# Output stage of an encoder layer: output products cut into quarters, with the transposes, routing and affinities of a tile between them

## The reference, cut to what matters

```python
    mixed = jnp.concatenate([out_a, out_b], axis=-1)
    x = x + jnp.matmul(mixed, w_o)
    x = x + expert_choice_moe(rmsnorm(x, norm2), w_router, w_gate, w_up, w_down)
...
    cap = CAPACITY_FACTOR * n_tok // N_EXPERTS
    aff = jax.nn.softmax(jnp.matmul(xt, w_router).astype(jnp.float32), axis=-1)
    gate, idx = lax.top_k(aff.T, cap)
    xg = xt[idx]
    h = jax.nn.silu(jnp.einsum('ecd,edf->ecf', xg, w_gate)) * jnp.einsum('ecd,edf->ecf', xg, w_up)
    y = jnp.einsum('ecf,efd->ecd', h, w_down) * gate[..., None].astype(x.dtype)
```

## Time and profile before

| | |
|---|---|
| median of 3 runs | 1774.64 us (1774.34 to 1776.37) |
| span of the profiled execution | 1773.7 us |
| PE busy in it | 1728.7 us, 97% |
| DVE, ACT, POOL busy | 1186.7, 1074.0, 388.9 us |
| mean clock granted to PE | 0.988 |

### The profile page before, as it was taken

How to read it: one execution, slowest core, us unless ns; L and a number is a source line. 1 busy time by engine, 2 the same in 40 slices (tenths; PEclk the granted TensorE clock), 3 DMA queues, 4 the chain that set the end, 5 groups by cost and what they waited for, 6 DMA issues and landing times.

```text
span 1773.7 us, 30258 instructions
## 1 busy us (share of the span) xinstructions
PE 1728.7 (97%) x10582; PEld 1576.8 (89%) x10582; DVE 1186.7 (67%) x2358; ACT 1074.0 (61%) x2140; POOL 388.9 (22%) x552
## 2 busy tenths in 40 slices
PE   9999999899999999999999999999999999999995
PEld 9789898799998878888899999999999999999994
DVE  4442533488888973137778777787777877778776
ACT  4333333388888983333466666666666666666665
POOL 1322402254445542221100111001110011100112
PEclk9999999899999999999999999999999999999998
DMA  7556645654544743334786786777867777777775
GB/s 236 125 160 202 192 126 153 161 165 149 149 147 134 208 117 127 110 107 152 253 271 245 267 272 226 263 251 266 269 228 259 256 266 258 239 254 260 267 265 227
DMA packets 203485, 367.13 MB, mean 207 GB/s; under 512 B 39055, under 2 KB 64655, under 8 KB 202831
## 3 DMA queue, kind: packets, MB, share of 16 engines
q1 hardware_dynamic: 190268, 320.92, 54.1%
q0 software_dynamic: 13120, 44.96, 9.9%
HBM read 321.67 MB, written 50.45 MB: 210 GB/s over the span
## 4 chain that ended last, share of the span: by engine, by line
PE 47%; DVE 2%; DMA 2%; ACT 1%; POOL 1%; issue 0%; DVEq 0%; SPq 0%; ACTq 0%; POOLq 0%
PE psum L2158 21%; PE psum L2160 10%; PE psum L2177 3%; PE psum L2178 3%; PE psum L2179 3%; PE psum L2180 3%; PE psum L2181 3%; PE psum L2143 1%; DMA own_rows<-x 1%; DMA x<-y_s,index 0%; DVE raw_weights L1858 0%; DMA rows_s<-xn,tokens 0%; DVE top_at L1442 0%; ACT xT_e L2022 0%; DVE affT L1444 0%
## 5 line engine op out<-in xcount | busy, mean ns | idle before, releaser
L2158 PE MATMUL psum<-x_parts,weight_parts 128*128 128x384 f32 x2048 | 583.5, 359 | 1.4 <-DVE x_parts L1836 1.4
L2160 PE MATMUL psum<-x_parts,weight_parts 128*128 128x192 f32 x2048 | 512.7, 250 | 0.0
L1791 DVE TENSOR_TENSOR weight_parts<-raw_weights,weight_parts 128x1024 fp32r<-128x1024 f32 x384 | 451.1, 1219 | 69.6 <-ACT weight_parts L1990 69.5
L1990 ACT ACTIVATE weight_parts<-raw_weights 128x1024 fp32r<-128x1024 f32 x384 | 381.8, 1055 | 23.2 <-DMA raw_weights<-in_w_gate 10.0
L2160 PEld LDWEIGHTS psum<-x_parts,weight_parts 128*128 128x128 f32 x2048 | 391.1, 191 | 0.6
L2158 PEld LDWEIGHTS psum<-x_parts,weight_parts 128*128 128x128 f32 x2048 | 384.4, 188 | 2.2 <-DVE x_parts L1836 1.6
L603 PE MATMUL psum<-x_hi,w_parts 128*128 128x512 f32 x624 | 193.5, 390 | 0.0
L1731 POOL DMA_INDIRECT x<-y_p,index x15 | 24.1, 1609 | 640.7 <-DVE y_s L1853 640.7
L2017 ACT ACTIVATE h_parts<-up_sum 128x192 fp32r<-128x192 f32 x128 | 46.6, 364 | 169.7 <-DVE up_sum L1806 169.6
L603 PEld LDWEIGHTS psum<-x_hi,w_parts 128*128 128x128 f32 x624 | 117.1, 188 | 26.9 <-issue 2.6
L842 POOL TENSOR_TENSOR logits_da<-logits_da 128x512 f32<-128x512 f32 (+1 forms) x96 | 103.9, 1104 | 159.1 <-DVE logits_da L928 159.1
(11 more groups left out here) (222 smaller groups left out, 3168.7 us busy)
## 6 DMA issues: line engine op xcount, KB each, us to landing
raw_weights<-in_w_gate SPq DMA_DIRECT2D x32, 2048.0 KB, 7.9
raw_weights<-in_w_up SPq DMA_DIRECT2D x32, 2048.0 KB, 9.4
raw_weights<-in_w_down SPq DMA_DIRECT2D x32, 2048.0 KB, 8.7
mixed<-in_w_in SPq DMA_DIRECT2D x96, 256.0 KB, 4.1
q_parts<-q SPq DMA_DIRECT2D x188, 128.0 KB, 3.0
bias_da<-da_rows SPq DMA_DIRECT2D x31, 512.0 KB, 4.1
q<-mixed POOLq DMA_DIRECT2D x96, 128.0 KB, 3.1
mixed<-in_x SPq DMA_DIRECT2D x12, 512.0 KB, 6.9
```

The costliest lines, as they stand in the source:

```text
L1791: dve.tensor_tensor(part_half(u, 1, half), src, part_half(u, 0, half).bitcast(F32), ALU.subtract).then_inc(split, 1)
L1990: act.activation(part_half(u, 0, half), src, ACT.Copy).then_inc(rounded, 1)
L2158: pe.matmul(out.rearrange("p (h n) -> p h n", h=2), w[:, 0, k, cols], x_parts[:, k, :, :], start=(k == 0), stop=False)
L2160: mm = pe.matmul(out[:, 0:SLOTS], w[:, 1, k, cols], x_parts[:, k, 0, :], start=False, stop=(k == KT - 1))
```

## The change: the order of work on PE, ACT and DVE in the output stage

A tile's product on PE is cut into quarters, q1 to q4 (half 0 and 1 of c = 0, then of c = 1; `product` takes `half`, 12 instructions each). The order of a tile's step becomes: q1, transposes of u's second half, q2, routing of u, q3, transposes of t's own first half, affinities of u, q4. Before it was: product c = 0, transposes of both halves of u, affinities of t - 2, product c = 1, routing of u. ACT's order follows it, and the normed rows of the last tile are written last of all. DVE does the softmax of u between the two adds of t, not behind them. The loop over tiles 4 to 7 is written out. After the last product, three and five `keep_busy` become fourteen in one place. The early rounds are 14, spread over tiles 8 to 11; affinities of the prompt's second half are written to rows 32 to 47 at once, so that the copy L1380 is gone. The eight late rounds are now six of the sample alone and two of both.

```diff
-EARLY_TOP_ROUNDS = 12
+EARLY_TOP_ROUNDS = 14
...
-                def product(t, i, c):
+                def product(t, i, c, half):
...
-                    for j in range(8):
+                    for j in range(4 * half, 4 * half + 4):
...
-                    mm.then_inc(products, 1)
+                    if half:
+                        mm.then_inc(products, 1)
...
                     if there(t):
-                        product(t, i, 0)
+                        product(t, i, 0, 0)
                         if there(u):
-                            transpose_rows(u, 1 - i)
-                        if there(v):
-                            transpose_affinities(v, i)
-                        product(t, i, 1)
-                        if is_last:
-                            transpose_rows(t, i)
+                            transpose_rows(u, 1 - i, 1)
+                        product(t, i, 0, 1)
                         if there(u):
                             route(u, 1 - i)
-                    elif there(u):
-                        route(u, 1 - i)
-                        keep_busy(pe, p, 1, 3)
-                        transpose_affinities(v, i)
-                    else:
-                        keep_busy(pe, p, 1, 5)
-                        transpose_affinities(v, i)
+                        product(t, i, 1, 0)
+                        transpose_rows(t, i, 0)
+                        if there(u):
+                            transpose_affinities(u, 1 - i)
+                        product(t, i, 1, 1)
+                    else:
+                        transpose_rows(u, 1 - i, 1)
+                        route(u, 1 - i)
+                        keep_busy(pe, p, 1, 14)
+                        transpose_affinities(u, 1 - i)
...
+                    if there(u):
+                        square(u, 1 - i)
+                        keep_hT(u, 1 - i, 1)
+                        if u != TILES - 1:
+                            normalize(u, 1 - i)
                         exponentiate(u, 1 - i)
                     if there(t):
-                        normalize(t, r, i)
-
-                pairs(act, step, 2)
+                        keep_hT(t, i, 0)
+                    if there(u):
+                        keep_affinities(u)
+                    if u == TILES - 1:
+                        normalize(u, 1 - i)
+
+                tiles(step, 1)
...
-                early = {9: (3, 0, 2), 10: (2, 0, 2), 11: (2, 1, 0)}
+                early = {8: (1, 2), 9: (2, 2), 10: (2, 2), 11: (2, 1)}
...
                         add_rows(t, i, 0)
+                    if there(t - 1):
+                        softmax(t - 1, 1 - i)
+                    if there(t):
                         early_rounds(t, 0)
                         add_rows(t, i, 1)
                         early_rounds(t, 1)
-                    if there(t - 1):
-                        softmax(t - 1, 1 - i)
-                    early_rounds(t, 2)
```

More of the change, by code:

```diff
@@ L1131, in col, with tiles @@
             return stats[:, i, c:c + width]
-        def routed_bank(t):
-            return bank(p, 0 if isinstance(t, int) and t == TILES - 1 else 6, EXPERTS)
-        def pairs(eng, step, lags=0):
-            for t in range(4):
-                step(t, t // 2, t % 2)
-            with eng.Fori(2, N_PROMPT // P // 2) as r:
-                for i in range(2):
-                    step(2 * r + i, r, i)
-            for t in range(N_PROMPT // P, TILES + lags):
+        routed_bank = bank(p, 6, EXPERTS)
+        def tiles(step, lags=0):
+            for t in range(TILES + lags):
                 step(t, t // 2, t % 2)
         def there(t):
-            return not isinstance(t, int) or 0 <= t < TILES
+            return 0 <= t < TILES
         def ge(eng, s, value):
-            if not isinstance(value, int) or value > 0:
+            if value > 0:
                 eng.wait_ge(s, value)
         def rows(v, t):
-            return v[bass.ds(t, 1)].rearrange("a p n -> (a p) n")
+            return v[t]
         with nc.Block() as block:
@@ L1199, in step @@
                     pool.tensor_tensor(col(i, 1), col(i, 0), p.minus_half[:, :], ALU.pow).then_inc(rstd_ready, 1)
-                pairs(pool, step)
+                tiles(step)
             @block.tensor
             def _(pe):
-                def product(t, i, c):
-                    if c == 0:
-                        if isinstance(t, int) and t == 0:
+                def product(t, i, c, half):
+                    if c == 0 and half == 0:
+                        if t == 0:
                             pe.wait_ge(first_mixed_split, 1)
@@ L1231, in route, with transpose_rows @@
+                def transpose_rows(u, iu, c):
+                    pe.wait_ge(summed, 2 * u + c + 1)
+                    ge(pe, hT_ready, 2 * u - 1 + c)
+                    for b in range(4):
+                        kt = 4 * c + b
+                        mm = pe.transpose(bank(p, 4 + c, P, b * P), x_res[:, iu, kt * P:(kt + 1) * P], p.ident[:, :])
+                    mm.then_inc(x_transposed, 1)
                 def route(u, iu):
                     pe.wait_ge(hT_ready, 2 * u + 2)
-                    if isinstance(u, int) and u == 0:
+                    if u == 0:
@@ L1316, in keep_affinities, with normalize @@
-                def keep_affinities(v):
-                    act.wait_ge(aff_transposed, v + 1)
-                    if isinstance(v, int) and v == 0:
-                        act.wait_ge(lists_cleared, 3)
-                    row, tile = 0, v
-                    if isinstance(v, int) and v >= N_PROMPT // P:
-                        half, tile = divmod(v - N_PROMPT // P, SAMPLE_HALF // P)
-                        row = (SAMPLE_ROW, SAMPLE_HALF_ROW)[half]
-                    act.activation(p.affT[row:row + EXPERTS, bass.ds(tile * P, P)], bank(p, 7, P)[0:EXPERTS, :], ACT.Copy
+                def normalize(u, iu):
+                    act.wait_ge(rstd_ready, u + 1)
+                    ge(act, xn_stored[iu], 16 * (u // 2))
+                    act.activation(xn[:, iu, :], x_res[:, iu, :], ACT.Copy, scale=col(iu, 1)).then_inc(normed, 1)
@@ new lines, in keep_affinities @@
+                def keep_affinities(u):
+                    act.wait_ge(aff_transposed, u + 1)
+                    if u == 0:
+                        act.wait_ge(lists_cleared, 3)
+                    row, first = ((0, 0), (HALF_ROW, HALF), (SAMPLE_ROW, N_PROMPT),
+                                  (SAMPLE_HALF_ROW, N_PROMPT + SAMPLE_HALF))[u // 4 if u < 8 else u // 2 - 2]
+                    at = u * P - first
+                    act.activation(p.affT[row:row + EXPERTS, at:at + P], bank(p, 7, P)[0:EXPERTS, :], ACT.Copy
@@ L1408, in step @@
                         early_rounds(t, 1)
-                    if there(t - 1):
-                        softmax(t - 1, 1 - i)
-                    early_rounds(t, 2)
-                pairs(dve, step, 1)
+                tiles(step, 1)
                 dve.wait_ge(aff_kept, TILES)
```

73 lines of the change are left out of this document (22 added, 51 removed).

## The result

The changed kernel took 1785.1 us in the median of 4 runs (1783.77 to 1787.06), the kernel before 1775.27 (1774.34 to 1776.37) on the same chip: ratio 1.0052 [1.0038, 1.0066], 9.8 us slower. The forecast was 1784.7.

A forecast was written before the change was run, and what follows sets the result against it. PE's list of work was taken to bound the output stage, then a latency chain to the first expert. Last product +8.45, tail +3.2, late rounds -1.6 gave +10.05, span 1783.75, plus 0.9: 1784.7 us; own range 1783.6 to 1786.2, wider 1781.0 to 1787.2.

The forecast's parts named there:

- The wait at the head: Tile 0's four transposes wait for DVE's first add, so PE issues nothing for 3.3 us: +3.3.
- The clock behind it: Behind the head's wait PE runs one 3.4 us stretch at half clock: +1.7, between nothing and 3.4.
- Thirteen more returns: Before the last product, 34 groups of other work instead of 21, 0.1 us per return to products: +1.3.
- Work ahead of the last product: Tile 10's routing and four transposes of tile 11 move ahead of PE's last product: +2.15.
- The tail: Last product to next stage's opening grows from 10.7 to 13.9 us, through fourteen `keep_busy` and a late store: +3.2.
- The late rounds: Two of eight late rounds go from 512 to 256 columns, 0.81 us less each: -1.6.
- Nothing for the early rounds, the copy and the loop: Two more early rounds, the dropped copy and the written-out loop lie under PE's products and cost nothing.
- The last step of the sum: Span 1783.75 us to run time 1784.7, taking the runs' median as 0.9 above the span.
- DVE did not fall behind: Rival: late DVE adds make PE wait in tiles 8 to 11, or the head loses more clock; 1786.4 to 1789, chance 0.14.
- the first transposes did wait: Rival denied here: tile 0's transposes do not wait at the head; +5.05, or +3.35 if the tail's clock holds; chance 0.06.
- PE's clock did not fall inside the tiles: Rival denied here: PE's clock halves for one stretch in each of twelve tiles, 20 us more, 1805; chance 0.02.
- The clock rival: Rival: the clock does not fall at the head, in the tail, or both; 1783.0 or 1781.2 us; chance 0.25.

The follow-up runs named there:

- e2: The changed kernel with thirteen useless products filling PE's wait before tile 0's first transposes; 1784.59 us, ratio 1.0045 to the kernel before.
- e6: The changed kernel with the affinities' transpose moved into the middle of the last quarter, one more return a tile; 1785.89 us, ratio 1.0055 to the kernel before.
- e3: The changed kernel with the last tile's normed rows written before its softmax; 1783.1 us, ratio 1.0038 to the kernel before.
- e4: The changed kernel with five `keep_busy` in the tail in place of fourteen; 1782.37 us, ratio 1.004 to the kernel before.
- e5: The changed kernel with the edits of e3 and e4 together; 1779.71 us, ratio 1.0024 to the kernel before.
- e8: The changed kernel with twelve early rounds in place of 14, two late rounds wide again; 1785.93 us, ratio 1.0061 to the kernel before.
- e10: The changed kernel with POOL's split of tile 1's `mixed` waiting until DVE has split `w_o`; 1783.51 us, ratio 1.0045 to the kernel before.
- e1: The changed kernel with tile 0's first-half transposes put back behind its whole product, into tile 1's step; 1780.35 us, ratio 1.0026 to the kernel before.
- e9: The changed kernel with e3, e10, tiles 0 to 6 transposed whole, and fewer `keep_busy`, placed in the tail's waits; 1772.44 us, ratio 0.9978 to the kernel before.
- the change twice: The changed kernel's first profile and that of its unedited repeat; medians 1785.1 and 1785.5 us, the repeat's ratio 1.0055 to the kernel before.

## Why the prediction was right

The steps, one by one, against the profile of the change.

- **The wait at the head: +3.3.** Tile 0's transposes came at F + 12.56. Before, product 37 was issued at 670.25, F + 9.28, and PE reaches the same point in the change at F + 9.32: 3.28 against before, 3.24 of it the wait itself.
- **The clock behind it: +1.7.** 1.74, by e2 against the change (1.67 of it at once).
- **Thirteen more returns: +1.3.** This term was mis-sized. What is left of Q's 169.18 - 161.25 = 7.93 after 3.28, 1.74 and the 2.15 below is 0.76, or 0.06 for each; e6 gives 0.07, the steps of the change against those before 0.04, so some of the 0.76 may belong to the term below. I had put down to the two returns all that a tile's step had over what its products take; a good third of it is something else.
- **Work ahead of the last product: +2.15.** It was not tested by itself. With it, the first three terms and e6's price (13 x 0.067 = 0.87) make 8.04, where 7.93 was measured.
- **The tail: +3.2.** B - Q is 14.10 and was 10.72: +3.38. The order of events was as forecast: half clock for one stretch, fourteen `keep_busy` to Q + 9.25 (forecast Q + 9.1), then the affinities, then the normed rows, and their store last. e3 took the store out of the chain (2.50), e4 most of the busy work (2.2 at A, 2.0 at B), and e5 both.
- **The late rounds: -1.6.** 16.40 against 17.99, and 18.00 with e8's rounds.
- **Nothing for the early rounds, the copy and the loop.** PE has no wait in tiles 1 to 11, and e8, with two rounds fewer, gains nothing there. DVE, with four rounds, is at 11.17 of 14 us, less than the 12.5 of the prediction. (The 12.25 of the earlier trace rows are no measure of this: nearly five rounds stand in that stretch.)

In sum +9.32 from F to E in the first profile, +9.88 in the second, +10.05 forecast. The returns were 0.54 too high and the tail 0.18 too low. Between G and E the two profiles differ by 0.56, and 0.48 of it is the gather of the sample's rows: PE waited 1.91 us for it in the first and 2.39 in the second.

The last step of the sum, 0.9 us from span to time, was misread: it set a median against the span of another execution. In the runs for which both are on record a run's time stands 1.7 to 2.3 us over its own span (1784.59 and 1782.7 in the profile of the change). This did no harm, since in effect the 10.05 was added to the median of the kernel before.

The rivals: DVE did not fall behind, the first transposes did wait, and PE's clock did not fall inside the tiles. The clock rival is not refuted. In its favour, the clock held behind the same hole in e6 and e10; it was I who had the wrong reason against it, for I took the one case of the earlier trace rows as a rule. In both profiles of the change it fell, so this rival did not come true there, but which of the two happens was not something that the profile of before could say. That the sum depends little on it was luck: of the five profiles with fourteen `keep_busy` and no fall at the head, four have two stretches at half clock in the tail (e1, e2, e6, e10), so that most of what the head saved was lost again, and the prediction had nothing of this.

## What to carry to other kernels

Work that waits for another engine must not stand in the midst of a bound engine's queue where the pipeline is still empty: a finer interleaving that costs 0.04 to 0.07 us a group in the steady state cost 5 us at the first tile. In a tail, put useless products into the waits and never between the last results and those who need them, and give the last store its place ahead of short work that nobody stores (e9: A at Q + 6.0 in place of Q + 9.25). A gain of one clock stretch at one place can be lost at the next, so read each edit's own marks in the trace beside the median.

## What the runs showed of the hardware that was not expected

**The same hole does not always cost the clock.** With PE idle 3.06 to 3.10 us behind 36 products, the granted clock fell to 0.50 for the next stretch in five profiles (the change twice, e3, e4, e5) and stayed at 1.00 in two (e6, e10); with 2.6 us it stayed (e8). In the five, PE had been busy 0.3 to 1.0 of the 3.4 us just before the fall, but e6 has a stretch as empty as that and no fall. In the tail the half clock lasts 3.4 us or 6.8, and with fourteen `keep_busy` it is 9.25 us from Q to A with the one (the change twice, e3, e8) and 10.87 to 10.90 with the other (e1, e2, e6, e10). The longer one stands only in profiles without a fall at the head, though e8 has neither. What decides it stays open. The moments at which the clock changes lie differently against the hole from profile to profile (in the five with a fall, it begins between F + 12.3 and F + 13.5, and the hole ends at F + 12.6); this is a rival to any account from the kernel's side, and no run set them or moved the place of the hole alone.

**DVE and POOL hold each other up.** In the change, DVE's first seven splits and POOL's one (DVE's timeline, then POOL's):

```profile
657.69 10.25 DVE L1341 TENSOR_TENSOR w_o_parts<-V,w_o_parts 128x1024 fp32r<-128x1024 f32 x7
```

```profile
662.28 3.45 POOL L1182 TENSOR_TENSOR mixed_parts<-mixed,mixed_parts 128x1024 fp32r<-128x1024 f32 x1 [8.89 <-ACT mixed_parts L1268]
```

One of the seven lasted 3.44 us, as long as POOL's; the eighth, alone, takes 1.21. In e1 it was the eighth that lasted 3.38 us, and the seven before it kept their pace (8.03 us), which is why they held PE up less. In e8 it went the other way, DVE's first, then POOL's:

```profile
659.25 6.90 DVE L1341 TENSOR_TENSOR w_o_parts<-V,w_o_parts 128x1024 fp32r<-128x1024 f32 x6
```

```profile
662.70 6.79 POOL L1182 TENSOR_TENSOR mixed_parts<-mixed,mixed_parts 128x1024 fp32r<-128x1024 f32 x1 [8.89 <-ACT mixed_parts L1268]
```

DVE's splits kept their pace (six in 6.90) and POOL's took 6.79, where it takes 2.35 in e10 and 2.4 in the tiles that follow. That moved tile 0's transposes from F + 12.56 to F + 11.03. The Trainium skill (SBUF — State Buffer, Who interferes with whom) says that the two engines share a pair of ports under an exclusive lock and that an instruction of DVE with both inputs in SBUF contends with an instruction of POOL that reads there. The rows agree that they hold each other up: in the change DVE's split lasted 2.2 us longer than alone (POOL's takes 2.35) and POOL's 1.1 longer (one of DVE's takes 1.2), and DVE's small scaling in e10 ended together with POOL's split. In e8 POOL's lost 4.4 us, more than three of DVE's splits. Which engine loses, and how much, differs from profile to profile of nearly the same code, and no run shows what decides it.
